# Decoder block with top-4-of-32 experts on one Trainium2 core: the first expert step's row list built on chip instead of read back from memory

## The chip, the cores and the metric

The kernel runs on one core of one Trainium2 chip. The metric is the device time of one execution in microseconds (us), median of the runs.

## What is computed

One decoder block over 1024 tokens of width 1024, in float32: a mixer (banded attention and a gated linear recurrence), then 32 experts of which each token uses four, then a norm. The change touches only the seam between the mixer and the experts. Of the reference, this is what is computed there:

```python
logits = (t @ w_router + b_router).astype(jnp.float32)
top_val, top_idx = lax.top_k(logits, TOP_K)          # TOP_K = 4 of 32
gate = jax.nn.softmax(top_val, axis=-1)
...
# per expert: xc = the rows of its tokens, in chunks
gu = xc @ w_gate_up[e] + b_gate_up[e]
g = jnp.minimum(gu[:, :D_EXPERT], 7.0); u = jnp.clip(gu[:, D_EXPERT:], -7.0, 7.0)
act = (u + 1.0) * (g * jax.nn.sigmoid(1.702 * g))
y = act @ w_down[e] + b_down[e]
out[token] += y * gate                               # then a residual add and RMSNorm
```

## The kernel before, in words

The program is written by hand, engine by engine: each engine has its own instruction stream, and semaphores tie them. Nothing reorders it; the order in each stream is the order of the text, and DMA transfers start where their engine comes to them.

**Tiles t = 0 to 7** (128 tokens each) go through the mixer's output product. For each tile, DVE makes the residual sum and the normed rows, which POOL writes to memory (`h2_rows`, printed h_rows by the profile). PE forms the router's logits (L639), DVE's `top(t)` (L1499 to L1509) picks four experts, PE's `rank(t)` (L648) counts how many earlier tokens chose each expert, and DVE's `place_rows(t)` (L1514 to L1524) turns that into a slot per token and choice: slot = expert * 1024 + rank. `slot_i` holds the slots, `entry` four words for each (token, gate, token * 4, 0).

**The slot table** `slot_tab` lies in memory, 1024 slots of 16 bytes per expert, filled beforehand with the token number 4096 (`FAR`), which no gather or scatter takes. POOL's `scatter(t)` (L1171) writes tile t's entries into it with four indirect DMAs of 128 entries each. After the last one (tile 7), POOL waits for all 32 scatters (`scattered`), reads the first 128 slots of expert 0 into `meta` (L1214), issues three loads of the final gain (L1217), waits for `meta`, and issues the gather of the 128 rows (`gather(0)`, L1198). PE waits for these rows and turns them (`rows_turn(0)`, L688).

**The step table** says which expert and chunk each step works on. DVE makes it from the counts per expert (L1560 to L1604), with PE's four transposes between (L682, released by `columns_done`). Every engine reads it (`table_done`) before it enters the loop over the steps.

**The loop over steps** j: a step is one chunk of up to 128 rows of one expert (tails of up to 32 rows ride along). A step has six weight units of 2 MB (units 0 to 3 gate and up, 4 and 5 down), cut into 24 pieces. For a piece, ACT copies the weights rounded to a shorter format (`w_hi`, L1019), DVE subtracts to get the rest (`w_lo`, L1617), and PE multiplies (L721, L722, L725). SP issues the unit loads (L389): units 4 and 5 of step 0 early, units 0 to 3 of step 0 back to back once the last tile's rows are stored, and each unit of a later step as soon as PE is done with it. POOL gathers step j + 1's rows during step j; PE turns them at piece 20.

The DVE stream at the seam ends with `top(7)`, `place_rows(6)`, `place_rows(7)` and the table. The scratch that it uses (`entry`, `slot_i`, the one-hot tables, the counts) lies in the ring where `w_lo` is later.

## Time and profile before

| | |
|---|---|
| Median of 3 runs | 2199.49 us (2197.26 to 2201.21) |
| The profiled execution | 2197.88 us, of which its span 2196.3 us |
| Last tile's slots ready (end of L1524) | 748.48 us |
| Last scatter issued, landed | 753.12 us, 764.36 us |
| First expert product (L721) | 779.60 us |
| PE busy over the span | 2039.7 us (93%) |

Times are microseconds from the start of the span. In a timeline row the first two numbers are start and duration, and the bracket says how long the engine sat idle before it and what ended that. "issue" and "remote" mean that the profile shows no instruction that ended the wait. Durations of DMA rows on POOL are the issue only; the transfer lands later.

### The profile page before, as it was taken

How to read it: one execution, taken by the hardware profiler on the slowest of the kernel's cores; microseconds unless marked ns; L12 is line 12 of the kernel's file. 1: busy time of each engine (PE TensorE's matmuls, PEld its weight loads, DVE VectorE, ACT ScalarE, POOL GpSimd, SP SyncE). 2: the span in 40 equal slices, each digit the busy share in tenths (PEclk: the TensorE clock that was granted, in tenths of full speed). 3: DMA queues.
4: the chain of work that ended last, by engine and by line, in shares of the span. 5: the costliest groups of instructions: out<-in, count | busy, mean ns of one | idle time of the engine just before them, and what ended most of it. 6: DMA issues, size and time to landing. Idle time of an engine off the chain costs nothing.

```text
span 2196.3 us, 37063 instructions
## 1 busy us (share of the span) xinstructions
PE 2039.7 (93%) x11768; PEld 1550.3 (71%) x11769; DVE 1596.5 (73%) x2052; ACT 1299.4 (59%) x1763; POOL 292.8 (13%) x334
## 2 busy tenths in 40 slices
PE   6989979999989489999999999999999999999993
PEld 5776657777768367777777777777777777777772
DVE  4766645555556477977977778987977988977894
ACT  5544435444543256766765667766756767765774
POOL 3100000000023411111211101111200111210000
PEclk9999989999999689999999999999999999999997
DMA  5030011010253767898977889978979979977994
GB/s 171 20 115 1 1 39 39 20 38 20 77 196 112 176 228 253 302 360 286 340 260 265 293 293 373 380 268 282 334 249 376 374 262 379 333 260 263 378 339 161
DMA packets 256004, 489.57 MB, mean 223 GB/s; under 512 B 20044, under 2 KB 38312, under 8 KB 255857
## 3 DMA queue, kind: packets, MB, share of 16 engines
q1 hardware_dynamic: 233824, 439.56, 55.9%
q0 software_dynamic: 21088, 49.35, 8.5%
q8 instruction: 30, 0.49, 0.1%
q14 instruction: 22, 0.17, 0.0%
q10 hardware_dynamic: 1040, 0.00, 0.0%
HBM read 461.01 MB, written 32.05 MB: 224 GB/s over the span
## 4 chain that ended last, share of the span: by engine, by line
PE 79%; DVE 8%; issue 5%; ACT 4%; DMA 2%; SPq 1%; POOL 0%; ACTq 0%; DVEq 0%; POOLq 0%
PE psum L721 15%; PE psum L722 14%; PE psum L725 14%; PE psum L738 8%; PE psum L562 3%; PE psum L564 3%; PE psum L566 3%; PE psum L445 3%; PE psum L447 2%; PE psum L446 2%; PE psum L709 2%; PE psum L542 2%; PE psum L688 1%; DVE o_lo L1450 1%; PE psum L749 1%
## 5 line engine op out<-in xcount | busy, mean ns | idle before, releaser
L1617 DVE TENSOR_TENSOR w_lo<-ring,w_hi 128x1024 fp32r<-128x1024 f32 x768 | 914.9, 1221 | 143.6 <-ACT w_hi L1019 131.8
L1019 ACT ACTIVATE w_hi<-ring 128x1024 fp32r<-128x1024 f32 x768 | 803.7, 1059 | 283.0 <-PE psum L725 264.3
L721 PE MATMUL psum<-w_hi,rows_hi 128*128 128x512 f32 x1024 | 422.4, 413 | 4.1 <-DVE rows_lo L1621 2.4
L722 PE MATMUL psum<-w_hi,rows_lo 128*128 128x512 f32 x1024 | 400.2, 391 | 0.0
L725 PE MATMUL psum<-w_lo,rows_hi 128*128 128x512 f32 x1024 | 316.7, 391 | 0.0
L721 PEld LDWEIGHTS psum<-w_hi,rows_hi 128*128 128x128 f32 x1024 | 193.9, 189 | 46.7 <-issue 10.2
L725 PEld LDWEIGHTS psum<-w_lo,rows_hi 128*128 128x128 f32 x1024 | 192.8, 188 | 41.2
L722 PEld LDWEIGHTS psum<-w_hi,rows_lo 128*128 128x128 f32 x1024 | 193.4, 189 | 37.7
L721 PE MATMUL psum<-w_hi,act_hi 128*128 128x512 f32 x512 | 219.8, 429 | 0.0
L722 PE MATMUL psum<-w_hi,act_lo 128*128 128x512 f32 x512 | 202.8, 396 | 0.0
L738 PE MATMUL psum<-ring,region_m 128*32 128x256 f32 x3072 | 174.2, 380 | 0.0
L725 PE MATMUL psum<-w_lo,act_hi 128*128 128x512 f32 x512 | 160.8, 395 | 0.0
L1247 POOL DMA_INDIRECT acc_rows<-region_m,meta x32 | 53.6, 1676 | 778.6 <-ACT region_m L1046 712.5
L738 PEld LDWEIGHTS psum<-ring,region_m 128*32 128x32 f32 x3072 | 96.2, 110 | 66.6 <-issue 7.2
L721 PEld LDWEIGHTS psum<-w_hi,act_hi 128*128 128x128 f32 x512 | 97.2, 190 | 22.3 <-issue 5.1
L725 PEld LDWEIGHTS psum<-w_lo,act_hi 128*128 128x128 f32 x512 | 96.1, 188 | 23.3
L722 PEld LDWEIGHTS psum<-w_hi,act_lo 128*128 128x128 f32 x512 | 96.7, 189 | 18.1
L875 ACT ACTIVATE g_hi<-ring,gmix 128x256 fp32r<-128x256 f32 x64 | 31.6, 506 | 113.6 <-PE psum L566 113.6
L1430 DVE SCALAR_TENSOR_TENSOR g_lo<-ring,gmix,g_hi 128x256 fp32r<-128x256 f32 x64 | 30.3, 484 | 91.6 <-ACT g_hi L875 91.5
L709 PE MATMUL psum<-region_s,region_m 96*128 96x512 bf16 (+1 forms) x384 | 89.1, 332 | 0.0
L562 PE MATMUL psum<-hT_hi,g_hi 128*128 128x512 f32 x256 | 80.2, 395 | 1.2 <-DVE g_lo L1430 1.2
L564 PE MATMUL psum<-hT_lo,g_hi 128*128 128x512 f32 x256 | 79.8, 393 | 0.0
(327 smaller groups left out, 3034.9 us busy)
## 6 DMA issues: line engine op xcount, KB each, us to landing
ring<-in_w_gate_up_dram SPq DMA_DIRECT2D x128, 2048.0 KB
ring<-in_w_down_dram SPq DMA_DIRECT2D x64, 2048.0 KB, 12.1
ring<-in_w_in_dram SPq DMA_DIRECT2D x16, 512.0 KB, 5.3
region_m<-in_x_dram SPq DMA_DIRECT2D x8, 512.0 KB, 11.7
ring<-in_w_in_dram SPq DMA_DIRECT2D x2, 2048.0 KB, 17.6
ring<-in_w_out_dram SPq DMA_DIRECT2D x2, 2048.0 KB, 7.6
region_a<-in_x_dram POOLq DMA_DIRECT2D x8, 512.0 KB, 4.2
acc_rows<-region_a POOLq DMA_DIRECT2D x8, 512.0 KB, 3.7
```

Source lines behind the costliest of these rows:

```text
L445: mm(dst, w_hi_, m_hi_, start=first, stop=False)
L562: mm(gate_bank(th, q), hi[:, cols], hT_hi[:, k, th * HALF:(th + 1) * HALF], start=first, stop=False)
L564: mm(gate_bank(th, q), hi[:, cols], hT_lo[:, k, th * HALF:(th + 1) * HALF], start=False, stop=False)
L566: last = mm(gate_bank(th, q), lo[:, cols], hT_hi[:, k, th * HALF:(th + 1) * HALF], start=False, stop=final)
L709: return mm(dst, sel_cur[0:96, u, 0:rows], bias3[0:96, BIAS_COL[i] + c:BIAS_COL[i] + c + width], start=False, stop=True)
L721: mm(bank(i), hi[:, ks], wh, start=(k0 + q == 0), stop=False)
L722: mm(bank(i), lo[:, ks], wh, start=False, stop=False)
L725: last = mm(bank(i), hi[:, (k0 + q) * P:(k0 + q + 1) * P], w_lo[:, buf, q * HALF:(q + 1) * HALF], start=False, stop=False)
L738: mm(dst[TAIL * q:TAIL * (q + 1), :], stat_of(k), wu[i][:, k, c:c + QC], start=(k == 0), stop=False)
L1019: act.activation(w_hi[:, n % NBUF, :], place[i][:, k0 * HALF:(k0 + 2) * HALF], ACT.Copy).then_inc(hi_done, 1)
L1247: g.indirect_dma_start(out=acc_rows, out_offset=bass.IndirectOffsetOnAxis(ap=meta[:, u, 0:1], axis=0), in_=yrow[u], in_offset=None, bounds ...
L1617: v.tensor_tensor(out=w_lo[:, n % NBUF, :], in0=place[i][:, k0 * HALF:(k0 + 2) * HALF], in1=w_hi[:, n % NBUF, :].bitcast(f32), op=ALU.subt ...
```

## The change

- **DVE** gets `first_rows(lo, hi)`: for each token of tiles lo to hi - 1, the smallest of its four slots (`first_at`), its gate if that slot lies in expert 0 (`first_w` summed into `first_row[..., 1]`), and a one-hot row of 128 columns that marks the slot (`first_hot`). It is called for tiles 0 to 5 ahead of `top(7)`, with one small instruction for the token numbers, and for tiles 6 and 7 after `place_rows(7)`.
- **PE** sums eight products (one per tile) of `first_hot` with `first_row` (token number less 4096, gate): 128 slots by 2 columns in bank 5. A slot that no token has comes out as 0, and DVE adds 4096. DVE's two copies put the result into `meta` for step 0, in place of the read from `slot_tab`.
- **POOL** waits for `first_meta`, gathers step 0's rows, and only then scatters tile 7, waits for all scatters and loads the final gain. The read L1214 and its wait are gone.
- **PE** turns step 0's rows ahead of the four transposes for the step table.
- **SP** issues units 0 and 1 of step 0 where it issued four, waits for step 0's rows, and issues units 2 and 3.
- `entry` and `slot_i` move to another place in SBUF, since the last scatter reads them while `w_lo` may be written; POOL makes one more constant (`iota_s`).

```diff
--- before.py
+++ after.py
@@ -218,8 +218,13 @@
             d_at[0] += n
             return ring[:, d_at[0] - n:d_at[0]]
 
-        entry = scratch(NT * TOPK * 4).bitcast(i32).rearrange("p (t k w) -> p t k w", t=NT, k=TOPK)
-        slot_i = scratch(NT * TOPK).bitcast(i32).rearrange("p (t k) -> p t k", t=NT)
+        entry = region_s[:, 3584:3584 + NT * TOPK * 4].bitcast(i32).rearrange("p (t k w) -> p t k w", t=NT, k=TOPK)
+        slot_i = region_s[:, 3584 + NT * TOPK * 4:3584 + NT * TOPK * 5].bitcast(i32).rearrange("p (t k) -> p t k", t=NT)
+        first_hot = scratch(NT * P).rearrange("p (t s) -> p t s", t=NT)
+        iota_s = scratch(P)
+        first_row = scratch(NT * 2).rearrange("p (t w) -> p t w", t=NT)
+        first_at = scratch(NT)
+        first_w = scratch(NT * TOPK).rearrange("p (t k) -> p t k", t=NT)
         mask_b = scratch(NE * NT // 2).bitcast(bf16).rearrange("p (t e) -> p t e", t=NT)
         oh4 = scratch(NT * TOPK * NE).rearrange("p (t k e) -> p t k e", t=NT, k=TOPK)
         at_slot = scratch(NT * NE).rearrange("p (t e) -> p t e", t=NT)
@@ -302,6 +307,7 @@
                              "count_mm", "table_done"))
         w_arrived = [sem(f"w_arrived{i}") for i in range(NU)]
         unit_mm = [sem(f"unit_mm{i}") for i in range(NU)]
+        first_built, first_mm, first_meta = sem("first_built"), sem("first_mm"), sem("first_meta")
         rank_read, rowsT_mm, rowsT_done, meta_in, tmeta_in, add_at_done = (
             sem(n) for n in ("rank_read", "rowsT_mm", "rowsT_done", "meta_in", "tmeta_in", "add_at_done"))
         rows_in, trows_in = [sem(f"rows_in{u}") for u in range(2)], sem("trows_in")
@@ -398,7 +404,10 @@
             for q in range(2):
                 sp.wait_ge(acc_out[q], 16 * (NT // 2))
                 sp.wait_ge(h2_out[q], 16 * (NT // 2))
-            for i in range(4):
+            for i in range(2):
+                unit(i, 0)
+            sp.wait_ge(rows_in[0], 16)
+            for i in range(2, 4):
                 unit(i, 0)
             sp.wait_ge(table_done, 1)
             with sp.Fori(0, MAXS) as j:
@@ -677,10 +686,10 @@
                 last = mm(bank(1)[:, 0:NE], ones_b[:], mask_b[:, s, :], start=(s == 0), stop=(s == NT - 1))
             last.then_inc(count_mm, 1)
 
-            pe.wait_ge(columns_done, 1)
-            for q in range(4):
-                last = tr(bank(0)[0:1, q * P:(q + 1) * P], tab_c[:, q:q + 1], ident[:])
-            last.then_inc(columns_mm, 1)
+            pe.wait_ge(first_built, 2)
+            for s in range(NT):
+                last = mm(bank(5)[:, 0:2], first_hot[:, s, :], first_row[:, s, :], start=(s == 0), stop=(s == NT - 1))
+            last.then_inc(first_mm, 1)
 
 
             def rows_turn(u):
@@ -695,6 +704,10 @@
             pe.wait_ge(slot_done, NT)
             pe.wait_ge(rows_in[0], 16)
             rows_turn(0)
+            pe.wait_ge(columns_done, 1)
+            for q in range(4):
+                last = tr(bank(0)[0:1, q * P:(q + 1) * P], tab_c[:, q:q + 1], ident[:])
+            last.then_inc(columns_mm, 1)
             pe.wait_ge(table_done, 1)
             total = pe.value_load(ends[0:1, 0:1], min_val=1, max_val=MAXS)
             pe.wait_ge(bias_done, 1)
@@ -1164,6 +1177,7 @@
             pool.wait_ge(pool_step, steps[0])
             g.iota(entry[:, :, :, 0], pattern=[[P, NT], [0, TOPK]], base=0, channel_multiplier=1).then_inc(entry_built, 1)
             g.iota(entry[:, :, :, 2], pattern=[[P * QUART, NT], [0, TOPK]], base=0, channel_multiplier=QUART).then_inc(entry_built, 1)
+            g.iota(iota_s, pattern=[[1, P]], base=0, channel_multiplier=0, allow_small_or_imprecise_dtypes=True).then_inc(entry_built, 1)
 
             def scatter(t):
                 pool.wait_ge(slot_done, t + 1)
@@ -1172,7 +1186,7 @@
                                          in_=entry[:, t, k, :], in_offset=None, bounds_check=NE * SEQ - 1,
                                          oob_is_err=False).then_inc(scattered, 16)
 
-            pool.wait_ge(entry_built, 2)
+            pool.wait_ge(entry_built, 3)
             pool.wait_ge(filled, 16 * (NE * SEQ // (P * FILL)))
             for t in range(NT):
                 pool.wait_ge(x2_done, t + 1)
@@ -1184,12 +1198,11 @@
                     g.dma_start(xb[t % 2], x_t[t + 2]).then_inc(xb_in[t % 2], 16)
                 if t >= 3:
                     scatter(t - 3)
-            for t in range(NT - 3, NT):
-                scatter(t)
+            scatter(NT - 3)
+            scatter(NT - 2)
             for q in range(2):
                 pool.wait_ge(acc_out[q], 16 * (NT // 2))
                 pool.wait_ge(h2_out[q], 16 * (NT // 2))
-            pool.wait_ge(scattered, 16 * NT * TOPK)
             chunks = slot_tab[0:NE * SEQ].rearrange("(c s) w -> c s w", s=P)
             quarters = slot_tab[P:].rearrange("(c s) w -> c s w", s=TAIL)
 
@@ -1211,12 +1224,13 @@
                                      in_offset=bass.IndirectOffsetOnAxis(ap=meta_t[0:TAIL, u, 0:1], axis=0),
                                      bounds_check=SEQ - 1, oob_is_err=False).then_inc(trows_in, 16)
 
-            g.dma_start(meta[:, 0, :], chunks[0]).then_inc(meta_in, 16)
+            pool.wait_ge(first_meta, 1)
+            gather(0)
+            scatter(NT - 1)
+            pool.wait_ge(scattered, 16 * NT * TOPK)
             for half in (slice(0, HALF), slice(HALF, 3 * QC), slice(3 * QC, D)):
                 signal = tadded if half.start == 3 * QC else added
                 g.dma_start(gfin[:, half], norm_final_g[None, half].to_broadcast([P, half.stop - half.start])).then_inc(signal, 16)
-            pool.wait_ge(meta_in, 16)
-            gather(0)
             pool.wait_ge(table_done, 1)
             total = pool.value_load(ends[0:1, 0:1], min_val=1, max_val=MAXS)
             _, _, tail, _, _, _, _ = load_step(pool, 0)
@@ -1236,7 +1250,7 @@
                             g.dma_start(meta[:, 1 - u, :], chunks[ds(e_next * (SEQ // P) + c_next, 1)].rearrange("a s w -> (a s) w")).then_inc(meta_in, 16)
                             with pool.If(t_next > 0):
                                 tail_rows(1 - u, e_next, c_next)
-                            wait_reg(pool, meta_in, j * 16 + 32)
+                            wait_reg(pool, meta_in, j * 16 + 16)
                             gather(1 - u)
                             with pool.If(t_next > 0):
                                 with pool.If(tail > 0):
@@ -1513,7 +1527,7 @@
                 dve.wait_ge(gexp_done, t + 1)
                 then(v.reciprocal(gsum[:, t:t + 1], gsum[:, t:t + 1]))
                 if t == 0:
-                    dve.wait_ge(entry_built, 2)
+                    dve.wait_ge(entry_built, 3)
                 v.tensor_tensor(out=entry[:, t, :, 1].bitcast(f32), in0=gate4[:, t, :], in1=bc(gsum[:, t:t + 1], [P, TOPK]), op=ALU.mult)
                 dve.wait_ge(rank_mm, t + 1)
                 v.scalar_tensor_tensor(out=at_slot[:, t, :], in0=iota_e[:], scalar=float(SEQ), in1=bank(7)[:, 0:NE],
@@ -1522,6 +1536,17 @@
                 then(v.tensor_tensor(out=oh4[:, t], in0=oh4[:, t], in1=bc(at_slot[:, t, None, :], [P, TOPK, NE]), op=ALU.mult))
                 then(v.tensor_reduce(out=slot_f[:, t, :], in_=oh4[:, t], axis=AX, op=ALU.add))
                 v.tensor_copy(slot_i[:, t, :], slot_f[:, t, :]).then_inc(slot_done, 1)
+
+            def first_rows(lo, hi):
+
+                ts = slice(lo, hi)
+                n = hi - lo
+                v.tensor_reduce(out=first_at[:, ts], in_=slot_f[:, ts, :], axis=AX, op=ALU.min)
+                then(v.scalar_tensor_tensor(out=first_w[:, ts, :], in0=slot_f[:, ts, :], scalar=float(SEQ),
+                                            in1=entry[:, ts, :, 1].bitcast(f32), op0=ALU.is_lt, op1=ALU.mult))
+                v.tensor_reduce(out=first_row[:, ts, 1:2], in_=first_w[:, ts, :], axis=AX, op=ALU.add)
+                v.tensor_tensor(out=first_hot[:, ts, :], in0=bc(iota_s[:, None, :], [P, n, P]),
+                                in1=bc(first_at[:, ts, None], [P, n, P]), op=ALU.is_equal).then_inc(first_built, 1)
 
             def merged_low(t):
                 dve.wait_ge(m_hi_done, t + 1)
@@ -1552,9 +1577,16 @@
                     place_rows(t - 3)
             top(NT - 2)
             place_rows(NT - 3)
+            v.tensor_scalar(first_row[:, :, 0], iota_t[:], iota_p, float(-FAR), ALU.add, ALU.add)
+            first_rows(0, NT - 2)
             top(NT - 1)
             place_rows(NT - 2)
             place_rows(NT - 1)
+            dve.wait_ge(slot_done, NT)
+            first_rows(NT - 2, NT)
+            dve.wait_ge(first_mm, 1)
+            v.tensor_scalar(meta[:, 0, 0:1], bank(5)[:, 0:1], float(FAR), None, ALU.add)
+            v.tensor_copy(meta[:, 0, 1:2].bitcast(f32), bank(5)[:, 1:2]).then_inc(first_meta, 1)
 
             dve.wait_ge(count_mm, 1)
             then(v.tensor_copy(cnt, bank(1)[:, 0:NE]))
```

The order of the instructions at the three places, word for word. **POOL**, from the last-but-one scatter on (slot_tab<- is a scatter, region_m<-h_rows the gather of rows, region_s<- the final gain). Before:

```order
L1171 DMA slot_tab<-ring 32896x4 [waits slot_done]
L1171 DMA slot_tab<-ring 32896x4 x3
L1171 DMA slot_tab<-ring 32896x4 [waits slot_done]
L1171 DMA slot_tab<-ring 32896x4 x3
L1214 DMA meta<-slot_tab 128x4 [waits h2_out1,acc_out1,scattered,h2_out0,acc_out0]
L1217 DMA region_s<-in_norm_final_g_dram 128x512
L1217 DMA region_s<-in_norm_final_g_dram 128x256 x2
L1198 DMA region_m<-h_rows,meta 128x1024 [waits meta_in]
L1221 TENSOR_LOAD ends [waits table_done]
```

After:

```order
L1185 DMA slot_tab<-region_s 32896x4 [waits slot_done]
L1185 DMA slot_tab<-region_s 32896x4 x3
L1211 DMA region_m<-h_rows,meta 128x1024 [waits h2_out1,acc_out1,first_meta,h2_out0,acc_out0]
L1185 DMA slot_tab<-region_s 32896x4 [waits slot_done]
L1185 DMA slot_tab<-region_s 32896x4 x3
L1233 DMA region_s<-in_norm_final_g_dram 128x512 [waits scattered]
L1233 DMA region_s<-in_norm_final_g_dram 128x256 x2
L1235 TENSOR_LOAD ends [waits table_done]
```

The gather moved ahead of the last four scatters and of the three loads, and the read of `meta` is gone.

**PE**, from the last rank product to the loop (psum<-ident,ring are the transposes for the table, psum<-ident,region_m those of the rows). Before:

```order
L677 MATMUL psum<-ring,ones_b 128x32 x8
L682 MATMUL psum<-ident,ring 1x128 [waits columns_done]
L682 MATMUL psum<-ident,ring 1x128 x3
L688 MATMUL psum<-ident,region_m 128x128 [waits rows_in0,slot_done]
L688 MATMUL psum<-ident,region_m 128x128 x7
L699 TENSOR_LOAD ends [waits table_done]
```

After:

```order
L686 MATMUL psum<-ring,ones_b 128x32 x8
L691 MATMUL psum<-ring 128x2 [waits first_built]
L691 MATMUL psum<-ring 128x2 x7
L697 MATMUL psum<-ident,region_m 128x128 [waits rows_in0,slot_done]
L697 MATMUL psum<-ident,region_m 128x128 x7
L709 MATMUL psum<-ident,ring 1x128 [waits columns_done]
L709 MATMUL psum<-ident,ring 1x128 x3
L712 TENSOR_LOAD ends [waits table_done]
```

Eight small products came in, and the table's transposes now stand behind the rows.

**DVE**, after the change, from the end of `place_rows(7)` to the start of the table:

```order
L1538 CAST region_s<-ring 128x4 [waits dve_step]
L1544 TENSOR_REDUCE ring<-ring 128x2 [waits slot_done]
L1545 SCALAR_TENSOR_TENSOR ring<-ring,region_s 128x8
L1547 TENSOR_REDUCE ring<-ring 128x2 [waits dve_step]
L1548 TENSOR_TENSOR ring<-ring 128x256
L1588 TENSOR_SCALAR meta<-psum 128x1 [waits first_mm]
L1589 COPY meta<-psum 128x1
L1592 COPY ring<-psum 128x32 [waits count_mm]
```

Before, the last of these (then L1560) followed the first (then L1524) directly; the work on the table now waits for PE's eight products.

## Rows read from the trace of the kernel before

**Rows 1.** Page, chain that ended last, by engine, whole span.
```profile
PE 79%; DVE 8%; issue 5%; ACT 4%; DMA 2%; SPq 1%; POOL 0%; ACTq 0%; DVEq 0%; POOLq 0%
```

**Rows 2.** Waits of PE, 780 to 2170 us: total, times, longest (us).
```profile
PE psum L749 <- DVE region_a L1646: 11.7, 16, 0.7
```

**Rows 3.** Chain in order of time, 753 to 780 us: start, duration, what.
```profile
753.12 11.23 DMA slot_tab<-ring
...
764.94 4.85 DMA meta<-slot_tab
...
770.61 4.47 DMA region_m<-h_rows,meta
...
775.21 1.96 PE psum L688 x8
...
777.19 1.03 ACT rows_hi L1011
...
778.24 1.23 DVE rows_lo L1621
...
779.60 0.79 PE psum L721
```

**Rows 4.** Timeline, DVE: start, duration, instruction, [idle before <- releaser].
```profile
738.35 0.19 DVE L1499 TENSOR_TENSOR region_a<-psum,brt 128x32 f32<-128x32 f32 x1 [2.18 <-issue]
...
747.44 0.19 DVE L1519 SCALAR_TENSOR_TENSOR ring<-iota_e,psum 128x32 f32<-128x32 f32 x1 [5.84 <-remote]
...
748.31 0.17 DVE L1524 CAST ring<-ring 128x4 int32<-128x4 f32 x1
...
748.93 0.19 DVE L1560 COPY ring<-psum 128x32 f32<-128x32 f32 x1 [0.45 <-remote]
...
754.66 0.15 DVE L1587 TENSOR_SCALAR ring<-ring 128x1 f32<-128x1 f32 x1
...
755.93 0.42 DVE L1590 COPY ring<-psum 1x264 f32<-1x264 f32 x1 [1.11 <-PE psum L682]
...
758.82 0.18 DVE L1604 CAST step_table<-ring 1x66 int32<-1x66 f32 x1
```

**Rows 5.** Timeline, POOL.
```profile
745.98 0.98 POOL L1171 DMA_INDIRECT slot_tab<-ring  x1 [0.31 <-issue]
...
749.28 0.98 POOL L1171 DMA_INDIRECT slot_tab<-ring  x1 [2.32 <-issue]
...
775.53 0.58 POOL L1236 DMA_DIRECT2D meta<-slot_tab  x1 [3.85 <-issue]
```

**Rows 6.** Timeline, PE.
```profile
734.69 3.62 PE L639 MATMUL psum<-wrt,region_a 128*128 128x32 f32 x16 [0.95 <-ACT region_a L962]
...
754.88 1.01 PE L682 MATMUL psum<-ident,ring 128*1 128x128 f32 x4 [13.65 <-issue]
```

**Rows 7.** Groups of DVE instructions, 700 to 800 us: busy us, mean ns.
```profile
L1522 DVE TENSOR_TENSOR ring<-ring 128x128 f32<-128x128 f32 x6 | 1.8, 292 | 0.2
```

**Rows 8.** Windows: busy us by engine, PE clock, DMA share, GB/s (last).
```profile
744.00:752.00 8.00, 0.00 (x0) 0.00 (x0) 3.45 (x19) 0.00 (x0) 4.46 (x6) 0.50 0.86 119
750.00:752.00 2.00, 0.00 (x0) 0.00 (x0) 1.65 (x10) 0.00 (x0) 1.39 (x3) 0.50 0.87 84
784.00:785.00 1.00, 1.00 (x4) 0.79 (x3) 1.00 (x2) 0.00 (x0) 0.00 (x0) 0.50 0.00 0
785.00:786.00 1.00, 1.00 (x6) 0.83 (x5) 0.27 (x2) 0.88 (x1) 0.00 (x0) 0.97 0.00 0
764.40:770.50 6.10, 0.00 (x0) 0.00 (x0) 0.00 (x0) 0.00 (x0) 2.25 (x4) 0.50 0.98 359
731.00:750.00 19.00, 7.13 (x57) 6.77 (x57) 7.45 (x40) 3.18 (x9) 12.65 (x13) 0.50 0.90 224
```

**Rows 9.** Line L1210 (gather of 32 rows, POOL), last row of its view.
```profile
DMA to landing us min/median/max: 2.8/3.5/6.7
```

**Rows 10.** Timeline, ACT: weight copy of piece 12, step 0.
```profile
795.23 1.06 ACT L1019 ACTIVATE w_hi<-ring 128x1024 fp32r<-128x1024 f32 x1 [0.55 <-PE psum L725]
```

## The prediction

> **What bounds the kernel now.** I read the page first: in the chain that ended last PE has 79% [rows 1]. Then the waits of PE in the loop over the steps: between 780 and 2170 us the largest is 11.7 us in all, sixteen waits of 0.7 us at most [rows 2]. So the loop runs at PE's pace, no weight or row is waited for, and what shortens the seam before it should move all that follows. The seam is read in the chain in order of time [rows 3]: the last scatter is issued at 753.12 and lands 11.23 us later; the read of the list takes 4.85; the gather 4.47; then PE turns the rows (1.96), ACT and DVE split them (1.03, 1.23) and the first product starts at 779.60. From the last tile's slots, ready at 748.31 + 0.17 = 748.48 [rows 4], to that product is 31.12 us, in which PE works for 3 us. The windows [rows 8] show why the scatter is slow: while scatters and weights share the DMA engines they move 84 to 119 GB/s in places, and 359 once the scatters have landed. The timelines show what else waits there: DVE stands 5.84 us before the last tile's L1519 [rows 4]; POOL issues its last scatters from 749.28 [rows 5].
>
> **The change, part by part.** The new path starts at the same 748.48.
>
> 1. `first_rows` of tiles 6 and 7 on DVE: three small instructions of 0.17 each, as L1524 [rows 4], and one comparison of 128x256. One of 128x128 takes 0.292 [rows 7]; twice that, 0.58, is an upper end, and I take 0.45, since a small one costs 0.17 already. With gaps 1.05: 749.5. The same for tiles 0 to 5 (128x768, some 1.0 us, and four small ones, 1.7 in all) stands ahead of `top(7)`, where DVE is idle for 2.18 [rows 4]. That covers it; without that cover it would cost at most 1.7.
> 2. Eight products on PE: no row has 128x128 weights with 2 columns. The nearest are the router's eight, 128x32: 3.62 us in sixteen records at the granted clock 0.50 [rows 6, 8]. Below stands twice the four transposes with one-column weights, 2 x 1.01 = 2.0 [rows 6]. The weights are those of the router's, so I take 3.55, and 0.15 to start: 753.2.
> 3. DVE's two copies out of PSUM, 0.19 each as L1560 [rows 4], and a gap: 753.7. POOL needs 0.8 from such a release to its DMA (748.48 to 749.28, [rows 4, 5]): the gather is issued at 754.5. POOL is free then: scatter 6 was issued by 745.98 + 0.98 [rows 5].
> 4. The gather: 4.47 [rows 3], behind the three gain loads, which are now behind it. The gather of 32 rows lands in 2.8 at best, 3.5 in the median [rows 9]. Its upper end is what the last scatter took, 11.23, if its queue is still full. I take 4.2, near its own row: 758.7. That needs the weights out of the way, and they are: 224 GB/s from 731 to 750 [rows 8] is 4.26 MB, the two units (4.19 MB) that SP now issues. By the Trainium skill (DMA: Bandwidth & Descriptors, on the anatomy of one DMA issued by GpSimd) a transfer takes about 2.0 us and its bytes at 436 GB/s. That is an estimate of 3.2 for these 512 KB, and the kernel's time would be 1.0 lower than mine; the row speaks against it.
> 5. PE turns the rows: 0.14 + 1.96 [rows 3]: 760.8. **What is late next is the step table.** DVE begins it at 753.8 where it began at 748.93, and needs 5.88 to the end of L1587 (754.81, [rows 4]): 759.7. That is 1.1 ahead of PE, which is behind the rows. The transposes take 1.01 [rows 6], DVE's second part 3.07 (755.93 to 759.00, [rows 4]): 764.9. Before, the table was done 16 us before the rows were turned; now the rows wait for it.
> 6. From the table to the first product PE reads two words and enters the loop, DVE reads one and makes `rows_lo`. Before, PE had 779.60 - 777.17 = 2.43 for its part, and `rows_lo` ended 0.13 before that [rows 3], so 2.43 is PE's upper end; the lower is 1.23, `rows_lo` alone. I take the upper: **767.3**.
>
> That is 12.3 us earlier. What else moves costs nothing as long as its cover holds. *Units 2 and 3* start at some 758.9. Unit 3 is first needed for piece 12, 795.23 - 779.60 = 15.6 after the first product [rows 10], at 782.9; the 4.19 MB need 11.7 us at 359 GB/s and 18.7 at 224 [rows 8], so they are there at 770.6 to 777.6. *Tile 7's scatters* are issued from 755.8 to 760.9 (1.28 apart, [rows 3, 5]) and land by 772 if the last takes 11.23 again. POOL then issues the gain loads (1.7), reads the table (3.85, [rows 5]) and starts step 1's list at 777.6; with 4.85 and 0.8 and 4.47 its rows are there at 787.7. PE turns them at piece 20, eight pieces of 1.3 after 782.9, so at 793. *The clock*: it is 0.50 until 785.0 and full from there [rows 8], 5.4 us after the first product; I assume the same again. At half clock a stretch costs double, so each us by which that rise moves is worth half a us; the two ends, rising at once or 5.4 later still, are a gain or a loss of 2.7.
>
> The sum: -12.3. The profiled execution took 2197.88 us (span 2196.3, 1.6 outside it) and lies 1.6 below the median, 2199.49, inside the range of the runs; I take the difference off the median: **2187.2 us**.
>
> **The rivals.**
>
> *A, DVE's stall does not come back.* The 5.84 us before L1519 have no releaser in the profile [rows 4]. If it was chance, or goes with four units in flight instead of two, the slots are ready at 742.6, and gather and table move along: up to 5.84 more, 2181.4 us. Against: all that precedes it in time is unchanged, weights and scatters are in flight as before. By the Trainium skill (Runtime: NRT & Kernel Launch, on instruction fetch) programs come in blocks of 256 instructions. Counted in DVE's order, exactly 768, three times 256, stand ahead of this L1519. By that rule the stall stays and comes five instructions of the old program earlier, on tile 6, and the time is my forecast; no row here shows a fetch.
>
> *B, the gather inherits the scatters' delay.* It goes in behind twelve scatters issued since 731, on the same queue. If it lands as late as the last scatter did, 11.23 after its issue, all is 7.0 later: first product at 774.3, gain 5.3, 2194.2 us. For: 11.23 was measured in that very queue. Against: then four units were in flight, 8.4 MB, until 770; now the second unit ends at about 750. The Trainium skill (same page on DMA, on queues, rings and completion order) says that a completion signal lands only after every earlier write of its engine, across queues. By that rule leftover scatters or weights hold the gather back; it names no time.
>
> *C, the other side: units 2 and 3 come too late.* They now run together with tile 7's scatters. At a rate r the 4.19 MB end at 758.9 + 4.19/r. At 119 GB/s, the window from 744 to 752 [rows 8], that is 794.1, 11.2 after piece 12 wants it: gain 1.1, 2198.4 us. At 84 GB/s (750 to 752) it is 808.8, 25.9 late: 13.6 slower, 2213.1 us. It breaks even where both take 36.3 us, at 115 GB/s. Against: only four scatters, not sixteen, are in flight, and even with sixteen the mean was 224 GB/s to 750.
>
> *D, the earlier start is given back* in the loop or the change's path isn't the one that the first product waits for: 2199.5 us. Against it stand PE's waits [rows 2].
>
> **Chances.** Forecast 0.55, A 0.17, B 0.13, C 0.09 (0.05 of it slower), D 0.06. About 0.2%, 4.4 us, is what a measurement of this kernel can tell from no change, so below 2195.1 is faster: the forecast, A, and 0.08 of B (at 2194.2 it is near the line) make 0.80; 0.05 of B, 0.04 of C and D make 0.15 same; 0.05 slower. The range goes from A with the shorter gather, 2181, to the late end of B with some spread of the runs, 2195.5; C and most of D stay out.
>
> **What would show it.** Right: the gather issued near 754.5 and landed near 758.7; PE's eight products 3.5 long; the first product near 767.3, released through the table and not through the rows; PE's later waits as before; piece 12's copy waiting for PE. Wrong: a gather of over 6 us (B), ACT waiting for unit 2 or 3 in step 0 (C), DVE without a stall before the last slots (A), a first product well before 780 with an end that is not earlier (D).

## The result: 5.9% slower, and the profile after

| | before | changed |
|---|---|---|
| Median | 2200.35 us (2197.26 to 2201.57, 4 runs) | 2330.33 us (2328.64 to 2331.48, 4 runs) |
| The profiled execution | 2197.88 us, span 2196.3 | 2329.47 us, span 2327.9 |
| Last tile's slots ready | 748.48 | 744.01 |
| First expert product | 779.60 | 769.00 |
| From it to the end of the span | 1416.7 | 1558.9 |

The ratio is 1.0593 (95% interval 1.0578 to 1.0608): 130 us slower, where 12.3 us faster was forecast. The last two lines of the table split it. The seam did become shorter, by 10.6 us; the 1416.7 us behind it, which the change doesn't touch, became 142.2 us longer.

First the seam, in the chain of waits of the changed kernel in order of time (start, duration, what); it answers to [rows 3].

```profile
749.61 10.89 DMA region_m<-h_rows,meta
...
760.64 1.94 PE psum L697 x8
762.58 0.87 PE psum L709 x4
...
763.48 0.43 DVE ring L1622
...
766.37 0.20 DVE step_table L1636
...
767.74 1.14 DVE rows_lo L1653
...
769.00 0.79 PE psum L734
```

Three timeline rows of DVE, then one of PE and one of POOL, answer to [rows 4 to 6]: the end of the last tile's slots (L1538), the comparison of `first_rows` over 768 and over 256 columns (L1548), the eight products (L691), the gather's issue (L1211).

```profile
738.12 0.95 DVE L1548 TENSOR_TENSOR ring<-ring 128x768 f32<-128x768 f32 x1
...
743.84 0.17 DVE L1538 CAST region_s<-ring 128x4 int32<-128x4 f32 x1
...
744.39 0.41 DVE L1548 TENSOR_TENSOR ring<-ring 128x256 f32<-128x256 f32 x1
...
744.86 3.58 PE L691 MATMUL psum<-ring 128*128 128x2 f32 x16 [2.18 <-DVE ring L1548]
...
749.61 1.06 POOL L1211 DMA_INDIRECT region_m<-h_rows,meta  x1 [0.71 <-issue]
```

The 5.84 us in which DVE stood [rows 4] are gone, the added work has the durations forecast, and the gather takes 10.89 us, not 4.2. The rows are turned at 760.64, and the step table's transposes (L709) follow directly: its columns were ready before, so the gather alone sets the time of both. What ran beside the gather, by DMA queue, from its issue to its landing (749.6 to 760.5; packets, MB, share):

```profile
q0 software_dynamic: 308, 0.53, 63.0%
q1 hardware_dynamic: 12, 0.02, 1.4%
```

Queue 1 carries the weights, queue 0 what POOL issues: the gather and the scatters. The weights had all but landed.

Then the loop. The page of the changed kernel: busy time, the queues that carry instructions, the chain by engine (it answers to [rows 1]), and the group of the loop's first product, with the idle time before it at the end.

```profile
PE 2082.8 (89%) x11784; PEld 1583.6 (68%) x11785; DVE 1601.6 (69%) x2063; ACT 1299.0 (56%) x1763; POOL 290.1 (12%) x334
...
q8 instruction: 159, 2.61, 0.5%
q14 instruction: 21, 0.17, 0.0%
...
PE 79%; issue 8%; DVE 7%; ACT 4%; DMA 1%; SPq 1%; POOL 0%; ACTq 0%; DVEq 0%; POOLq 0%
...
L734 PE MATMUL psum<-w_hi,rows_hi 128*128 128x512 f32 x1024 | 435.9, 426 | 99.6 <-issue 94.0
```

The same lines of the kernel before:

```profile
q8 instruction: 30, 0.49, 0.1%
...
L721 PE MATMUL psum<-w_hi,rows_hi 128*128 128x512 f32 x1024 | 422.4, 413 | 4.1 <-DVE rows_lo L1621 2.4
```

A row of a queue gives packets, MB and share. Queue 8 brings instructions: 30 packets before, 159 now, 16 KB each (2.61 MB by 159). PE's waits in the changed kernel, from 780 us to the end (answers to [rows 2]: total, times, longest):

```profile
PE psum L734 <- issue: 111.1, 21, 7.8
PE psum L762 <- DVE region_a L1678: 7.5, 11, 0.7
```

No weight, row or engine is waited for more than before; PE waits 111.1 us for nothing that the profile names, and it is busy for 43.1 us more over the span (2082.8 and 2039.7), of which the eight products are 3.6. One such wait, with the windows around it (us, busy by engine, PE's granted clock, DMA share, GB/s) and the DMA queues from 1050 to 1060:

```profile
1055.00 0.79 PE L734 MATMUL psum<-w_hi,rows_hi 128*128 128x512 f32 x1 [7.16 <-issue]
```

```profile
1040.00:1047.00 7.00, 7.00 (x74) 4.57 (x76) 5.75 (x5) 5.93 (x7) 1.12 (x1) 1.00 1.05 387
1055.00:1058.00 3.00, 3.00 (x7) 2.42 (x8) 0.00 (x0) 0.04 (x1) 0.00 (x0) 0.50 1.05 392
...
1058.00:1059.00 1.00, 1.00 (x3) 0.72 (x3) 0.00 (x0) 1.00 (x1) 0.39 (x1) 0.50 1.05 395
1059.00:1060.00 1.00, 1.00 (x4) 0.82 (x3) 0.95 (x1) 0.02 (x1) 0.57 (x2) 0.67 1.06 410
1060.00:1061.00 1.00, 1.00 (x6) 0.83 (x5) 0.41 (x2) 0.79 (x1) 1.00 (x3) 1.00 1.04 385
```

```profile
q8 instruction: 2, 0.03, 2.0%
```

PE stands 7.16 us, two blocks of instructions arrive, and its clock, full before, is half for another 4.7 us, which costs 2.3: some 9.5 us each time. The loop over the steps is passed 16 times in this run (two steps a pass). The first pass brings six packets in either kernel. Of the other fifteen, fourteen bring some nine each in the changed kernel, and one, from 1243.1 to 1340.7, brings none, has no such wait and is as long as before (97.6 us and 97.5). The 142.2 us are thus 10.2 for each of the fourteen; the four regular ones from 850 to 1243 took 9.1 to 9.3 more than before.

### The profile page after: what moved, and what is told of

It reads as the page before. It is cut to its first block, busy times and chain, and to the rows that moved or that the text cites. A ratio compares the mean times of both kernels' runs of the same rounds, so it can differ in the third digit from the quotient of the medians.

```text
span 2327.9 us, 37137 instructions
## 1 busy us (share of the span) xinstructions
PE 2082.8 (89%) x11784; PEld 1583.6 (68%) x11785; DVE 1601.6 (69%) x2063; ACT 1299.0 (56%) x1763; POOL 290.1 (12%) x334
## 3 DMA queue, kind: packets, MB, share of 16 engines
q8 instruction: 159, 2.61, 0.5%
## 4 chain that ended last, share of the span: by engine, by line
PE 79%; issue 8%; DVE 7%; ACT 4%; DMA 1%; SPq 1%; POOL 0%; ACTq 0%; DVEq 0%; POOLq 0%
PE psum L734 15%; PE psum L735 14%; PE psum L738 14%; PE psum L751 7%; PE psum L571 3%; PE psum L573 3%; PE psum L575 3%; PE psum L454 3%; PE psum L456 2%; PE psum L455 2%; PE psum L722 2%; PE psum L551 1%; DVE o_lo L1464 1%; PE psum L673 1%; PE psum L697 1%
## 5 line engine op out<-in xcount | busy, mean ns | idle before, releaser
L734 PE MATMUL psum<-w_hi,rows_hi 128*128 128x512 f32 x1024 | 435.9, 426 | 99.6 <-issue 94.0
L735 PE MATMUL psum<-w_hi,rows_lo 128*128 128x512 f32 x1024 | 412.5, 403 | 0.0
L738 PE MATMUL psum<-w_lo,rows_hi 128*128 128x512 f32 x1024 | 325.3, 400 | 0.0
L734 PEld LDWEIGHTS psum<-w_hi,rows_hi 128*128 128x128 f32 x1024 | 202.1, 197 | 146.4 <-issue 107.3
L738 PEld LDWEIGHTS psum<-w_lo,rows_hi 128*128 128x128 f32 x1024 | 199.2, 195 | 43.7
L735 PEld LDWEIGHTS psum<-w_hi,rows_lo 128*128 128x128 f32 x1024 | 201.3, 197 | 39.9
```

What stands on the lines that cost most here:

```text
L734: mm(bank(i), hi[:, ks], wh, start=(k0 + q == 0), stop=False)
L735: mm(bank(i), lo[:, ks], wh, start=False, stop=False)
L738: last = mm(bank(i), hi[:, (k0 + q) * P:(k0 + q + 1) * P], w_lo[:, buf, q * HALF:(q + 1) * HALF], start=False, stop=False)
```

## The theory and its rivals

**P, the place of PE's loop.** In the compiled program PE's part of the loop is 1629 instructions. The Trainium skill (Runtime: NRT & Kernel Launch, on instruction fetch) says that programs are fetched in blocks of 256 instructions, 16 KiB; the packets here are 16 KB each (2.61 MB by 159), and a loop of 1629 is 6.4 such blocks. It began at PE's instruction 6223 before and 6255 in the changed kernel: the eight f32 products are 32 instructions. By where it starts, such a loop touches seven blocks or eight. If seven stay at hand and eight don't, the loop is fetched again when it is passed again. The 30 packets of the kernel before would then be its whole program, 7854 instructions or 30.7 blocks, once.

The count alone doesn't say which kernel is slow. A loop of 1629 reaches into an eighth block when it starts at place 164 to 255 of a block; counted from the program's first instruction, 6223 is place 79 and 6255 is place 111, and both would touch seven. The theory needs the blocks' edges to lie 53 to 68 instructions off this count. That number is fitted to two runs below (fast when moved by 16, slow by 32), and nothing else here shows it.

**R1**, something the change *does* slows the loop: two units fetched later, the arrays' new places, other semaphores. **R2**, more instructions cost in proportion. The runs put instructions that compute nothing into PE's program, in either kernel: semaphore increments (`pe.sem_inc(reg_seen)`) at its start, or small products into a bank that nothing reads.

## Experiments: the loop

**before_pad32.** The kernel before; ahead of PE's first wait only this is added:

```
+            for _ in range(32):
+                pe.sem_inc(reg_seen)
             pe.wait_ge(ident_built, 1)
```

> The kernel before, with nothing changed but 32 semaphore increments on PE ahead of its first wait, where PE is idle for 9.97 us. They move PE's loop over the steps by 32 instructions, as the eight new products of the change do (each is two weight loads and two matmuls in the trace). Theory P (place of PE's loop): the loop is about 1629 instructions, 6.4 blocks of 256, and moved by 32 it reaches into one block more and is fetched anew on every pass. Then this kernel shows the loss of the change without the change: 141 us more in the loop, about 2340 us, and some 159 packets in the instruction queue q8 instead of 30. Theory S (the seam: the deferred units, the order of scatter and gather, or the moved buffers upset the loop): 2200 us and 30 packets.

Measured: 2337.05 us (2333.26 to 2341.67) against 2196.49, ratio 1.0638 (1.0618 to 1.0658). Its page and its waits of PE from 860 us on:

```profile
q8 instruction: 168, 2.75, 0.5%
```

```profile
PE psum L723 <- issue: 107.7, 19, 7.8
```

32 instructions that compute nothing, with no other part of the change, give the whole loss in the loop (1557.5 us from the first expert product to the end, 1558.9 in the changed kernel). R1 falls.

**before_pad176.** The same with `range(176)`.

> The kernel before, with 176 semaphore increments on PE ahead of its first wait. Theory P: 176 move the loop past the end of a block, so that it lies inside as few blocks as before: 2200 us (up to 5 more if the increments outlast PE's idle start), q8 near 30 packets. A rival to P, that more instructions on PE cost time wherever they lie: slower than the kernel with 32.

Measured: 2215.03 us (2212.8 to 2216.86), ratio 1.0083 (1.0066 to 1.01), 31 packets. That is 10 us above what was put down, and the loss is ahead of the loop: PE's program reached its first product at 28.05, the increments being that long, and the first expert product came at 798.21, 1416.0 us before the end. More instructions than in before_pad32 and no loss in the loop: R2 falls.

**before_pad16** and **before_pad60**: `range(16)`, `range(60)`, one run each.

> The kernel before with 16 semaphore increments on PE, half of 32. Theory P says that there is a step and no slope: either as before (2197 us, q8 near 30) or the whole loss (2337 us, q8 near 160). A cost that grows with the number of instructions: 70 us more.

> The kernel before with 60 semaphore increments on PE. Theory P: the loop is 28 instructions further into the same block position that cost 141 us at 32 and is still within it: 2337 us, q8 near 160. If the loss at 32 was tied to one exact place (a branch target on a block's edge, say), the kernel is as fast as with 16: 2197 us.

Measured: 2194.16 us and 30 packets with 16; 2330.79 us and 143 packets with 60.

**before_pad96, before_pad128, before_pad288**, one run each, to see whether the band of bad places has the width and the period that seven or eight blocks would give.

> The kernel before with 96 increments at the start of PE's program. P (a loop of 1629 instructions is 6.36 blocks of 256; it touches seven or eight blocks by where it starts, and is fetched anew on each of sixteen passes where it touches eight): eight blocks are touched from 92 or 93 of 256 starting places. Slow begins between 17 and 32 instructions, so it lasts to between 108 and 124, and 96 is slow: 2325 to 2340 us, 140 to 170 packets of the instruction queue, 1550 to 1562 us from the first product to the end. Rival (the slow band is narrower and ends soon after the 60 that was measured): 2197 to 2205 us, 31 packets, 1416 us from the first product.

> As before_pad96, with 128 increments. P: 128 lies past the end of the slow band (108 to 124), so the loop is fast again: 31 packets, 1416 to 1418 us from the first product; the increments themselves (0.163 us each, 20.9 in all) push PE's start back and the end to some 2200 to 2208 us. Rival (the band reaches up to 143): 150 packets or so and 1550 us or more from the first product.

> As before_pad96, with 288 = 256 + 32 increments. P: the same place in a block as with 32, one block later, so slow: 150 to 170 packets, 1550 to 1562 us from the first product, whatever the late start of PE costs ahead of it (47 us of increments, some 37 more than PE's start allows, of which most may show). Rival (what matters is the length of the program ahead of the loop or something that 144 instructions have passed for good): 31 or 32 packets and 1416 us from the first product.

Measured, with the others, by how far the loop's start is moved:

| moved by | kernel | packets of queue 8 | first product to end, us |
|---|---|---|---|
| 0 | before | 30 | 1416.7 |
| 16 | before_pad16 | 30 | 1416.4 |
| 32 | changed kernel | 159 | 1558.9 |
| 32 | before_pad32 | 168 | 1557.5 |
| 60 | before_pad60 | 143 | 1549.9 |
| 96 | before_pad96 | 105 | 1560.3 |
| 128 | before_pad128 | 31 | 1422.8 |
| 144 | after_pad112 | 31 | 1424.5 |
| 176 | before_pad176 | 31 | 1416.0 |
| 176 | after_pos144 | 31 | 1417.2 |
| 288 | before_pad288 | 160 | 1550.0 |

The instruction queue on the pages of 96, 128 and 288, in this order:

```profile
q8 instruction: 105, 1.72, 0.3%
```

```profile
q8 instruction: 31, 0.51, 0.1%
```

```profile
q8 instruction: 160, 2.62, 0.5%
```

A loop of 1629 touches eight blocks from 92 of 256 starting places. The band of slow places begins between 17 and 32 and ends between 97 and 128; from the first edge, 108 to 124 was computed for the second. 288 is 256 + 32 and is slow again. That there is a band is shown. A width of 92 and a period of 256 fit all eleven rows, but by themselves the runs leave 65 to 111 for the width, and the return of the loss rests on one run. That seven blocks stay and eight don't is worked out from this fit. A full pass brings nine packets, one more than the eight blocks that it touches; no run explains the ninth.

With 96 the time, 2346.54 us, was 6.5 above the range put down, as its first expert product came 5 us late (784.56), ahead of the loop; its 105 packets are fewer than the 140 put down. 128 took 2215.74 us, 8 above its range and again ahead of the loop, and 288 took 2367.07. Packets fall from 168 to 105 as the start moves through the band, and the time doesn't. Pass by pass the trace of before_pad96 shows how: its passes bring two, five, six or nine packets, and one with two (973.3 to 1065.9, one wait of 5.1 us) is still 6.4 us longer than before. So the price goes with the wait and not with the number of packets; why fewer blocks come, I can't say. The 6 to 8 us by which 128 and 144 stand above 1416 are one wait in the first pass (5.20 us, `issue`, at 807.83 in after_pad112) and the half clock behind it, up to 813; that a first fetch falls at a worse place there is a guess.

The Trainium skill (Runtime: NRT & Kernel Launch, on instruction fetch) says that PE holds 2048 instructions, eight blocks, and elsewhere in that section that a taken branch to outside the current two pages forces a fetch. By the second, the kernel before would fetch on each pass; its 30 packets speak against it. By the first, a loop in eight blocks would stay; 159 packets speak against that. The limit in these runs lies between the two.

## Experiments: the seam

**after_pad112.** The changed kernel with `range(112)` at the start of PE's program, its loop moved out of the band.

> The changed kernel, with 112 semaphore increments on PE ahead of its first wait: with the 32 new instructions the loop is 144 further than before, past the end of a block. Theory P: the 141 us are gone and the earlier first product (769.0 in place of 779.6 us) is left: 2189 us, q8 near 30 packets. Theory S: 2330 us, as the change.

Measured: 2199.18 us (2196.41 to 2202.51), ratio 1.0012 (1.0002 to 1.0021), 31 packets. The increments made PE start at 18.28 us instead of 10.05, and that lateness lay on the path up to the seam: the last slots were ready at 753.13. So this run shows the loop mended, and hides what the seam gained; the 2189 us put down were missed by 10.

**after_pad112_all4.** SP issues all four units at once, as the kernel before does.

```
-            for i in range(2):
-                unit(i, 0)
-            sp.wait_ge(rows_in[0], 16)
-            for i in range(2, 4):
+            for i in range(4):
                 unit(i, 0)
```

> As after_pad112, but SP issues units 0 to 3 of step 0 back to back, without the wait for step 0's rows: one part of the change undone. The gather took 10.89 us with two units in flight. If the weights in flight hold it back, it takes longer here, up to 20 us, and the time is up to 10 us above after_pad112 (2190 to 2200). If the scatters ahead of it on its own queue hold it back, it takes 11 us as there and the time is the same.

Measured: 2204.52 us (2201.05 to 2205.59), ratio 1.0033 (1.0021 to 1.0046). Holding two units back is thus worth 5.3 us here. The gather takes 12.64 us where it took 9.18, from the same issue (758.82 and 758.74), and 1.9 MB of weights go beside it, where there were none:

```profile
758.82 12.64 DMA region_m<-h_rows,meta
```

**after_pos144.** The changed kernel with 60 increments at the start, which PE's first wait hides, and 42 small products (84 instructions) where PE waits for step 0's rows anyway; the loop is 144 further than in the changed kernel.

```
+            for _ in range(60):
+                pe.sem_inc(reg_seen)
...
+            for _ in range(42):
+                mm(bank(3)[:, 0:NE], ones_b[:], tri_b[:, 0:NE], start=True, stop=True)
             pe.wait_ge(slot_done, NT)
             pe.wait_ge(rows_in[0], 16)
             rows_turn(0)
```

> The changed kernel with the loop moved by 144 instructions without cost: 60 semaphore increments ahead of PE's first wait (60 of the 0.163 us measured with 112 fit into PE's first 9.97 us idle) and 42 tiny products (84 instructions) while PE waits 12 us for step 0's rows. The loop stands where it stood in before_pad176, which ran its first pass without the 5.2 us fetch wait that after_pad112 had in step 0. Theory P: the first product at 769 to 770, the loop 1416.5 us from there to the end as before, 2187 us, about 10 below the kernel before. If the seam itself gives back in the loop what it gains (units 2 and 3 late, rival C): after_pad112's 1424.5 us again, 2195.

Measured: 2184.89 us (2182.8 to 2186.92), ratio 0.9949 (0.9937 to 0.9961), 11.1 us faster than the kernel before beside it (2195.96). This is the change as it was meant: 1.2 us short of the gain predicted (12.3), and 2.3 below the time predicted, as the kernel before ran 3.5 us faster beside it than in the prediction's runs. Its chain:

```profile
750.85 8.74 DMA region_m<-h_rows,meta
...
759.72 1.94 PE psum L699 x8
...
768.07 0.79 PE psum L738
```

**after_pos144_one.** SP issues one unit ahead of the gather, three behind it: `range(1)` and `range(1, 4)` in place of `range(2)` and `range(2, 4)`.

> As after_pos144, with SP issuing unit 0 alone ahead of the rows, and units 1 to 3 behind them. The gather took 10.9 and 9.2 us with two units in flight and 12.7 with four. If weights in flight hold it back, it is shorter here, 4 to 7 us, and the first product 3 to 6 us earlier: 2182 to 2184 us, unless unit 1, due at piece 4, comes late, which gives it back. If the scatters ahead of it do, 10 us and no change.

Measured: 2181.21 us (2179.24 to 2185.68), ratio 0.9938 (0.9925 to 0.9951). The gather again, and the first product:

```profile
748.19 5.76 DMA region_m<-h_rows,meta
754.09 1.94 PE psum L699 x8
...
762.45 0.79 PE psum L738
```

**after_pos144_cols.** The table's transposes stand ahead of the wait for the rows again, so that the table is made while the gather runs:

```
+            pe.wait_ge(columns_done, 1)
+            for q in range(4):
+                last = tr(bank(0)[0:1, q * P:(q + 1) * P], tab_c[:, q:q + 1], ident[:])
+            last.then_inc(columns_mm, 1)
             pe.wait_ge(slot_done, NT)
             pe.wait_ge(rows_in[0], 16)
             rows_turn(0)
-            pe.wait_ge(columns_done, 1)
...
```

> As after_pos144, with PE's four transposes for the step table ahead of the rows again, as they were before the change. In the changed kernel DVE had the table's columns at 754.5 and the rows came at 760.5; so the table is ready before the rows. If the table behind the rows is what the first product waits for, this gives the 4 us between rows_lo's earliest (763.7) and its actual start (767.7): 2183 us. If something else binds, no change from after_pos144.

Measured: 2181.14 us (2179.28 to 2183.28), ratio 0.9935 (0.9923 to 0.9947); the gather takes 9.37 and the first product comes at 763.17. PE's idle time before it is 2.45 us, where it was 5.56 in after_pos144.

**after_pos144_cols_one.** Both.

> after_pos144 with both edits that were 4 us better alone: the table's transposes ahead of the rows, and unit 0 alone issued ahead of them. With one unit ahead the rows came at 754.0 and the table at 759.99; with the transposes first the table should be done at 757 to 758, just behind the rows' 756.0 to 758: the first product at 759.5 to 761, 2177 to 2179 us. If the two edits remove the same wait, 2181 us as each alone.

Measured: 2181.09 us (2178.77 to 2182.31), ratio 0.9927 (0.9914 to 0.9941): no more than either alone. The first product is the earliest of all, 761.72, but the chain then goes through the second weight unit, which now waits for the rows, and ACT waits for it (the chain's row, and the waits of ACT from 765 to 830):

```profile
757.61 15.88 DMA ring<-in_w_gate_up_dram
```

```profile
ACT w_hi L1036 <- DMA ring<-in_w_gate_up_dram: 10.5, 3, 7.6
```

By PE's second products of L766 the 1.45 us are given back: 793.05 here, 793.08 in after_pos144_cols. This is rival C's mechanism with one unit ahead instead of two. The three versions at 2181 us beat both kernels and can't be told from one another here.

**after_pos144_scatter_first.** The gather stands behind tile 7's four scatters; the list is still built on chip.

> after_pos144 with the gather behind the last tile's four scatters (POOL's order before the change) and still without waiting for them. The gather is issued 5.1 us later (four issues of 1.28). If it lands when its queue is drained, it is 5 us later and the time 2190 us; if it only waited for the weights in flight, which are in by then, it lands almost as early: 2186 us.

Measured: 2187.55 us (2185.83 to 2189.22), ratio 0.9956 (0.9941 to 0.9971), 2.7 us above after_pos144. The gather is issued 10.79 us behind the slots (753.94, they were ready at 743.15) and not 5.60, and takes 7.84. The order of scatter and gather is worth 2.7 (2.0 if each is taken against the kernel before beside it); counted from the slots, 4.3 (27.1 us to the first product, not 22.8). What is left of the gain, 9.1 against 2196.66, belongs to the list's not going through memory and to the two units held back together. No run tells the two apart here; the nearest price of the units alone is the 5.3 us of after_pad112_all4.

**before_again.** The kernel before, unchanged, for a second profile.

> The kernel before, unchanged, for a second profile. DVE's 5.84 us ahead of the last tile's L1519 was in the first profile and not in those of before_pad16, before_pad32 and before_pad176, whose DVE programs are the same. If it belongs to this program (to where PE's or DVE's instructions stand), it is here again, 5 to 6 us; if it was chance, it is not, and the first product stands near 776 us.

Measured: 2197.36 us. DVE doesn't stand at the last tile: its slots are ready at 744.49, four us earlier than in the first profile. But POOL issues the last scatter at 753.09, as before (753.12), since its sixteen scatters go 1.28 us apart, and the chain from there is that of [rows 3]:

```profile
753.09 11.30 DMA slot_tab<-ring
...
764.98 4.95 DMA meta<-slot_tab
...
770.75 4.32 DMA region_m<-h_rows,meta
...
779.59 0.79 PE psum L721
```

## Why the prediction was wrong

**The step that failed** is the first one, ahead of the sum: "the loop runs at PE's pace, no weight or row is waited for, and what shortens the seam before it should move all that follows". It took the loop's 1416.7 us as fixed. The eight products were charged 3.55 us of PE's time, which is right (3.58), and nothing for being 32 instructions in a program whose loop stood 17 to 32 places from the edge of a band. That is worth +142.2 us, against -10.6 of everything else. No rival held it; A to C spoke of the seam's waits, and D named the loop without a mechanism in it. I had counted blocks of 256 for DVE's stall and not for PE, the engine that sets the pace and whose loop is longest. "No row here shows a fetch" was true of the rows printed and not of the page of the profile: its queue of instructions, 30 packets, was there to read.

The seam's steps, from the slots (748.48 forecast, 744.01 measured):

- *Step 1, 2, 3* held. The comparison of 768 took 0.95 (1.0), that of 256 0.41 (0.45), the products 3.58 (3.55); the gather was issued 5.60 behind the slots (6.02).
- *Step 4* was mis-sized: 10.89 us, not 4.2. "The weights out of the way, and they are" held: their queue moved 0.02 MB beside the gather. What the sum left out is **B**, and B's size, 11.23, came close. The gather stands behind twelve scatters in the same queue, and they were still landing. The last of them, issued at 747.92, has this row:

```profile
DMA to landing us min/median/max: 11.7/11.7/11.7
```

So it landed at 759.6, and the gather at 760.50. The same pair is 758.4 and 759.59 in after_pos144, 760.0 and 761.78 in after_pos144_scatter_first, 769.2 and 771.46 in after_pad112_all4; with the scatters all landed the gather takes 4.32 (before_again). The units still matter: the gather took 12.64 us with four issued ahead, 7.84 to 10.89 with two, 5.76 and 7.01 with one. With two or fewer next to no weights went beside it (0.37 MB at most), so they must act earlier, by holding the scatters back; that is argued, as the landings of the scatters with one unit are not in the traces. The prediction's own row, 4.47, came from behind landed scatters. The Trainium skill (DMA: Bandwidth & Descriptors, on the anatomy of one DMA issued by GpSimd) gave the estimate of 3.2 for the same transfer, and no run came below 4.29 (before_pad32). Its rule on completion signals (same page, on queues, rings and completion order) does not account for the delay in the trace of the changed kernel: the gather's last 4 KB packet itself ends 10.32 us after the issue, and its packets take 0.83 us each, 0.20 in before_again. Whether the order in the queue or the scatters' writes in memory slow them, no run tells.
- *Step 5* held in its claim (the table, not the rows, is late next) but not in its reason: DVE's columns were to be 1.1 ahead of PE and were ready at 754.5, six us before the rows; only the transposes' place behind the rows in PE's order made the table late. Undoing that order gives 3.8 us (2184.89 to 2181.14), 3.3 if counted from the slots (22.8 and 19.5 us to the first product). *Step 6* held: first product 2.4 behind the table's end.
- **A**: the stall isn't there. It comes and goes: the same program had it once and once not (before_again), so its place in blocks of DVE's instructions, by which I had put it down as lasting, does not explain it. The count was off as well: 838 instructions of DVE stand ahead of this L1519 in the trace, its semaphore instructions among them, and not 768. PE's product for this L1519 was done at 741.01, so PE did not hold it. Such stalls, with no releaser, stand in three more traces of the kernel before, at this line or the next copy: 4.37 and 4.61 us in before_pad96, 7.27 in before_pad128 and in before_pad288. What causes them stays open. Its absence gave 4.47 us of the 5.84, and it is no gain against a usual run of the kernel before, whose scatters hide it (before_again). With B's 6.7 us it nearly cancels: first product 10.6 earlier, not 12.3. That this comes so close is luck.
- **C** did not come with two units ahead; it came, small, in after_pos144_cols_one, with one. **D**'s words, an earlier start given back in the loop, describe the result best, with a price nearly twelve times too small (12.3 for 142.2) and the wrong reason: it was to be a path that doesn't bind.
- *The clock* rose at 773.0, 4.0 behind the first product (5.4 forecast), worth under 1 us. In the loop it is what makes each fetch dearer than its wait.

With the loop moved out of the band the time is the one predicted, 2184.89 against 2187.2 us, and the gain 11.1 against 12.3; that is luck in part, as the gather landed 4.5 us late and the slots were ready 3.2 us early.

## What to carry to other kernels

When an edit adds or removes instructions ahead of a long loop on the engine that sets the pace, read the instruction queue's packets in the profile first of all: more of them than the program has blocks of 256 means a loop that is fetched again. The count of blocks says how wide the band of bad places should be, and not where it lies; runs with some instructions more tell that. Such a loss is a step and not a slope, has nothing to do with what the added instructions do, and is undone by some tens more of them put where the engine waits anyway. A small gather costs what still stands ahead of it in its queue, so take its price from a row with the same queue ahead, and hold weights back only as far as the next piece allows.

## What the runs showed of the chip that I had not expected

- A loop of 1629 instructions on PE is free of fetches or costs some 10 us in nearly every pass by its starting place alone: 6% of the kernel for 32 instructions.
- A wait of 7 us for instructions halves PE's granted clock for some 4.7 us more.
- A semaphore increment on PE takes 0.155 us: with 288 of them PE's first product came at 45.43, with 176 at 28.05.
- A gather of 512 KB took 4.3 us with nothing ahead of it in its queue and 10.89 behind twelve scatters of 2 KB, with no weights beside it.
- DVE stands 4 to 7 us, with no releaser in the profile, in some executions of the same work and not in others, without a change of the total where the scatters hide it.
